# Routing of a mixture of experts: one number for each token, one-hots over the main blocks alone, and the first gathers inside the routing

## What is computed

```python
g_sel = jnp.argmax(g_logits, axis=-1)                  # one of 8 groups
top_p, top_i = lax.top_k(e_prob, 2)                    # two of its 8 experts
gate = g_gate * top_p / jnp.sum(top_p, axis=-1, keepdims=True)
expert = g_sel[:, None] * 8 + top_i
...
hb = jax.nn.silu(xb @ w1[e]) * (xb @ w3[e])            # xb: the rows of expert e
y = hb @ w2[e]
...
out = out.at[tok].add(y * gate)                        # each token gets two rows back
```

## Time and profile before

| | us |
|---|---|
| median of 3 runs | 3280.99 |
| lowest and highest | 3271.0, 3282.21 |
| the profiled execution | 3282.73 |
| its span, first to last instruction | 3280.9 |
| mean granted TensorE clock in it | 0.939 |

### The profile page before, as it was taken

One profiled execution on the slowest core, in us unless ns is written; L12 is line 12 of the kernel. 1 busy time (PEld: TensorE's weight loads), 2 busy tenths in 40 slices (PEclk: granted clock), 3 DMA queues, 4 the chain that ended last, 5 costly groups with the idle time before them and its releaser, 6 DMA issues. The chain is left out here.

```text
span 3280.9 us, 43057 instructions
## 1 busy us (share of the span) xinstructions
PE 2813.0 (86%) x16709; PEld 1832.8 (56%) x16709; DVE 1559.1 (48%) x2502; ACT 940.7 (29%) x1565; POOL 322.1 (10%) x388
## 2 busy tenths in 40 slices
PE   5999879897999999999999997698878766988785
PEld 3678778575888878865555576233222552333231
DVE  3148868558777766764555556011111571111114
ACT  6112322244322324444333432011001451111014
POOL 0000045300000000120101000111100001111100
PEclk8999989898999999999999997899999978999897
DMA  7511100212322338550000125899999759999996
GB/s 290 204 56 38 65 14 1 116 52 77 109 97 96 109 107 276 189 178 7 7 7 4 52 94 209 366 399 424 424 423 416 268 200 378 399 424 424 423 415 254
DMA packets 196700, 663.63 MB, mean 202 GB/s; under 512 B 42039, under 2 KB 83070, under 8 KB 142734
## 3 DMA queue, kind: packets, MB, share of 16 engines
q1 hardware_dynamic: 178062, 627.26, 49.0%
q0 software_dynamic: 18432, 33.60, 2.7%
HBM read 614.36 MB, written 79.95 MB: 212 GB/s over the span
## 5 line engine op out<-in xcount | busy, mean ns | idle before, releaser
L3131 PE MATMUL psum<-moe_ring,hreg 128*32 128x512 f32 x2976 | 482.8, 633 | 90.1 <-DMA moe_ring<-in_moe_w 48.2
L3131 PEld LDWEIGHTS psum<-moe_ring,hreg 128*32 128x32 f32 x2976 | 146.6, 116 | 386.4 <-issue 319.7
L3131 PE MATMUL psum<-x,hreg 128*32 128x512 f32 x896 | 319.8, 650 | 13.4 <-DMA moe_ring<-in_moe_w 13.4
L3237 DVE TENSOR_TENSOR ex_hb<-ex_sil,psum 128x256 f32<-128x256 f32 x64 | 27.0, 422 | 577.9 <-ACT ex_sil L3210 577.9
L3183 PE MATMUL psum<-moe_ring,hreg 128*32 128x512 f32 x1344 | 221.9, 599 | 16.6 <-issue 14.6
L1351 PE MATMUL psum<-gu_hi,x1r 128*128 128x512 f32 x712 | 226.6, 394 | 7.9 <-DVE x1r L1478 3.8
L1704 PE MATMUL psum<-dn_op 128*128 128x512 f32 x924 | 212.7, 393 | 4.3 <-DVE dn_op L1799 4.3
L1704 PEld LDWEIGHTS psum<-dn_op 128*128 128x128 f32 x924 | 175.3, 190 | 41.7 <-DVE dn_op L1799 5.1
L3210 ACT ACTIVATE ex_sil<-psum 128x256 f32<-128x256 f32 x64 | 24.6, 385 | 566.8 <-PE psum L3131 566.8
L1351 PE MATMUL psum<-gu_hi,gu_er 128*128 128x512 f32 x504 | 158.5, 389 | 0.0
L1351 PEld LDWEIGHTS psum<-gu_hi,x1r 128*128 128x128 f32 x712 | 135.4, 190 | 37.8 <-DVE gu_lo L1474 7.4
(11 more groups left out here) (643 smaller groups left out, 5893.3 us busy)
## 6 DMA issues: line engine op xcount, KB each, us to landing
moe_ring<-in_moe_w SPq DMA_DIRECT2D x256, 1024.0 KB, 19.2
x<-in_moe_w SPq DMA_DIRECT2D x96, 1024.0 KB, 21.6
moe_top<-in_moe_w SPq DMA_DIRECT2D x24, 1024.0 KB, 21.0
x<-in_w_down SPq DMA_DIRECT2D x77, 256.0 KB, 3.0
x<-midrow SPq DMA_DIRECT2D x77, 256.0 KB, 3.5
XF<-in_w_ada SPq DMA_DIRECT2D x16, 1024.0 KB, 6.2
moe_ring<-yrow SPq DMA_DIRECT2D x16, 1024.0 KB, 10.2
xrow<-x SPq DMA_DIRECT2D x24, 512.0 KB, 3.5
```

Of the source, the lines that this page charges most:

```text
L3131: last = pe.matmul(ps[i][r, :], xT[i][:, k, r], place[HOME[n, j]][:, kk * 512:(kk + 1) * 512], start=k == 0, stop=k == KD - 1)
L3237: dve.tensor_tensor(hb[i][:, :], sil[q % 2][:, :], ps[i][:, DE:2 * DE], ALU.mult).then_inc(hbd, 1)
```

## The change

Five things are changed in `routing`, and the parts that go with them.

- **One number for each token.** The constant table `C_TAB` goes. TensorE adds one more product to the sum in `ps[2]`: `code`, a constant of the rank, times `ranked_at`, a one-hot of each expert's rank. So `ps[2]` holds the token's rank in its low ten bits, and the place of its expert and the passes of its window above them. VectorE multiplies and sums once for each choice instead of twice, cuts the number into five fields with shifts and masks (`FI`, `F`), and block and row are sums of fields. A token without a place gets a block number out of range.
- **One-hots over 32 blocks.** The block one-hots of all 16 groups are made by one operation (`BO`, 512 columns), and two more weigh them with the two parts of the token's number (`BV`). They and the 16 row one-hots are bf16, each with a buffer of its own, so that nothing waits for a buffer. ScalarE makes none of them. TensorE has 16 bf16 products of 64 columns where 16 f32 ones of 96 were.
- **Overflow apart.** What served the further blocks alone (`Vrow`, `OC`, their one-hots and lists) moves to the new `overflow_routing`, under the same `nc.If`. `F` and `ovc` stay allocated until behind it, and so do the routing's buffers; the top places of the ring are named behind it.
- **First gathers.** The four first gathers are issued by GpSimd at the end of the routing block, when the list is there and the buffers are zeroed. `ranked_experts` starts with the fifth. The overflow branch issues them once more at its end, because it uses their buffers.
- **Idle products.** `keep_busy(pe, K, 0, 3)` ahead of the first turn goes. The gates' arithmetic (`GT`) moves from behind the one-hots to a place ahead of them.

```diff
+def gather(pool, K, q, place, sem):
+    pool.indirect_dma_start(place, None, K.xrow, bass.IndirectOffsetOnAxis(ap=K.GIDX[:, q:q + 1], axis=0),
+                            bounds_check=L - 1, oob_is_err=False).then_inc(sem, 16)
...
             @block.gpsimd
...
+                pool.wait_ge(zeroed, 4)
+                pool.wait_ge(gidx_ok, 1)
+                for q, xg in enumerate(gather_buffers(K)):
+                    gather(pool, K, q, xg, K.ga[q])
...
             @block.tensor
...
+                    if t == 2:
+                        pe.wait_ge(over_ok, 1)
+                        pe.matmul(ps[1][:, 0:NE], one[0:NE, :], over_it[:, :], start=True, stop=True).then_inc(over_mm, 1)
...
+                pe.wait_ge(at_ok, 1)
+                pe.matmul(ps[2][:, :].rearrange("p (t e) -> p t e", e=NE), code[:, :],
+                          ranked_at[:, :].unsqueeze(1).to_broadcast([P, NT, NE]), start=False, stop=True).then_inc(cmm, 1)
...
-                    pe.matmul(ps[6][:, 0:NB], RO[n % 4][:, :], BO[n % 4][:, :], start=n == 0, stop=n == 2 * NT - 1).then_inc(tmm, 1)
+                    last = pe.matmul(ps[6][:, 0:2 * MAIN], RO[:, n, :], BV[:, n, :, :].rearrange("p v b -> p (v b)"),
+                                     start=n == 0, stop=n == 2 * NT - 1)
...
             @block.vector
...
+                dve.tensor_scalar(ranked_at[:, :], ps[1][:, 0:NE], cst[:, C_COL + 2:C_COL + 3], None, ALU.is_equal).then_inc(at_ok, 1)
...
+                dve.tensor_tensor(BO[:, :, :], iota(MAIN).unsqueeze(1).to_broadcast([P, 2 * NT, MAIN]),
+                                  blf[:, :].unsqueeze(2).to_broadcast([P, 2 * NT, MAIN]), ALU.is_equal)
...
+                for n in range(2 * NT):
+                    dve.tensor_scalar(RO[:, n, :], numbers[:, :], rwf[:, n:n + 1], None, ALU.is_equal).then_inc(oh_ok, 1)
...
+                dve.tensor_single_scalar(K.GIDX[:, 0:MAIN], K.SIDX[:, 0:MAIN], 1, ALU.arith_shift_right).then_inc(gidx_ok, 1)
...
 def ranked_experts(nc, K, A, layer, tag, ctx, E):
...
-        for q in range(NG + passes[0]):
-            gather(q)
+        for q in range(NG, NG + passes[0]):
+            rows(q)
...
-        keep_busy(pe, K, 0, 3)
         turn_x(0)
...
 def moe(nc, K, A, layer, R, after):
...
         with nc.If(overflow > 0):
+            overflow_routing(nc, K, f"or{layer}_", R)
             experts(nc, K, A, layer, f"ov{layer}_", MAIN, OVER, [K.sem(f"ov{layer}_w{s}") for s in range(4)], 0)
```

More of the change, by code:

```diff
@@ L117, in constant_table @@
     t[:NE, C_COL + 1] = e
+    t[:, C_COL + 2] = i % NE
+    t[:NE, C_COL + 3] = 1024 * (e % GROUPS + GROUPS * np.array(FIRST_PASS)[e // GROUPS])
+    t[NE:, C_COL + 3] = 131072 * (passes - 1)
+    for k in range(2):
+        for m in range(NT):
+            t[:, C_VAL + 2 * (k * NT + m)] = 2 * i + k + 1
+            t[:, C_VAL + 2 * (k * NT + m) + 1] = 256 * m
     return t
@@ L2809, in routing @@
-        one, before = sb("one", [P, P], BF16), sb("before", [P, P], BF16)
-        sli, rwi, bli = (sb(n, [P, 2, NT], I32) for n in ("sli", "rwi", "bli"))
-        rwf, blf, nbl = sb("rwf", [P, 2, NT]), sb("blf", [P, 2, NT]), sb("nbl", [P, 2, NT])
-        ntk = sb("ntk", [P, 2 * NT])
-        RO = [sb(f"RO{i}", [P, P]) for i in range(4)]
-        BO = [sb(f"BO{i}", [P, NB]) for i in range(4)]
-        vt, v0 = sb("vt", [P, NB]), sb("v0", [P, NB])
-        BA = [sb(f"BA{n}", [P, NB]) for n in range(7)]
@@ L2817, in routing @@
-        exd, rmm, oh_ok, tmm, ones_ok = (K.sem(tag + n) for n in ("exd", "rmm", "oh_ok", "tmm", "ones"))
-        before_ok, cmm, block_ok, act_ok = (K.sem(tag + n) for n in ("before_ok", "cmm", "block_ok", "act_ok"))
-        by_act = range(3, 2 * NT, 2)
-        rank_ok, order_mm, order_ok, v_ok, v_mm, oe_ok, eo_mm = (K.sem(tag + n) for n in (
-            "rank_ok", "order_mm", "order_ok", "v_ok", "v_mm", "oe_ok", "eo_mm"))
+        one, before, code, numbers = (sb(n, [P, P], BF16) for n in ("one", "before", "code", "numbers"))
@@ L2852, in _ @@
                 for t in range(NT - 1):
-                    last = pe.matmul(ps[2][:, (t + 1) * NE:NT * NE].rearrange("p (t e) -> p t e", e=NE), one[:, :],
-                                     AS[:, t:t + 1, :].to_broadcast([P, NT - 1 - t, NE]), start=False, stop=t == NT - 2)
-                last.then_inc(cmm, 1)
+                    if t == 2:
+                        pe.wait_ge(over_ok, 1)
+                        pe.matmul(ps[1][:, 0:NE], one[0:NE, :], over_it[:, :], start=True, stop=True).then_inc(over_mm, 1)
@@ new lines, in _ @@
+                    pe.matmul(ps[2][:, (t + 1) * NE:NT * NE].rearrange("p (t e) -> p t e", e=NE), one[:, :],
+                              AS[:, t:t + 1, :].to_broadcast([P, NT - 1 - t, NE]), start=False, stop=False)
+                pe.wait_ge(code_ok, 1)
+                pe.wait_ge(at_ok, 1)
+                pe.matmul(ps[2][:, :].rearrange("p (t e) -> p t e", e=NE), code[:, :],
+                          ranked_at[:, :].unsqueeze(1).to_broadcast([P, NT, NE]), start=False, stop=True).then_inc(cmm, 1)
@@ L2871, in _ @@
+                last.then_inc(tmm, 1)
             @block.scalar
@@ L2966, in _ @@
+                dve.tensor_copy(blf[:, :], bli[:, :])
                 dve.drain()
[L2967 to L2974 removed]
@@ L3044, in ranked_experts @@
     hb = [sb(f"hb{i}", [P, DE]) for i in range(4)]
-    ga = [K.sem(tag + f"ga{i}") for i in range(NG)]
+    ga = K.ga
     sc = [K.sem(tag + f"sc{i}") for i in range(NY)]
@@ L3095, in gpsimd @@
                 for q in range(start[x + 1], end[x + 1]):
-                    gather(q + NG)
+                    rows(q + NG)
             for q in range(start[x], end[x]):
@@ L3343, in carry_wait, with gather_block @@
                     pool.tensor_tensor(scr[:, 0:1], scr[:, 1:2], scr[:, 1:2], ALU.add)
-                def gather(b, p, half):
+                def gather_block(b, p, half):
                     wait(pool, tx, b, -1, 2)
@@ L3376, in _ @@
                     pool.wait_ge(sc[i], 16 * count // 2)
+                for q, place in enumerate(gather_buffers(K)):
+                    gather(pool, K, q, place, rnew)
+                pool.wait_ge(rnew, 64)
             @block.tensor
@@ L3505, in moe @@
         K.last_in = [K.sem(f"moe{layer}_last{k}") for k in range(2)]
+        K.ga = [K.sem(f"moe{layer}_ga{i}") for i in range(len(gather_buffers(K)))]
+        chosen = ExitStack()
+        K.F = chosen.enter_context(nc.sbuf_tensor(f"moe{layer}_F", [P, 5, 2 * NT], F32))
+        K.ovc = chosen.enter_context(nc.sbuf_tensor(f"moe{layer}_ovc", [NE, 1], F32))
         routing(nc, K, A, layer, f"ro{layer}_", R)
-        R.ctx.close()
-        for i in range(AT_TOP):
-            with nc.sbuf_tensor(f"moe{layer}_top{i}", [P, PIECE], F32, side="right") as under:
-                K.place.append(under[:, :])
         overflow = nc.values_load(K.EO[0:1, OVER:OVER + 1], min_val=0, max_val=OVER)
@@ L3517, in moe @@
         with nc.If(overflow > 0):
+            overflow_routing(nc, K, f"or{layer}_", R)
             experts(nc, K, A, layer, f"ov{layer}_", MAIN, OVER, [K.sem(f"ov{layer}_w{s}") for s in range(4)], 0)
+        chosen.close()
+        R.ctx.close()
+        for i in range(AT_TOP):
+            with nc.sbuf_tensor(f"moe{layer}_top{i}", [P, PIECE], F32, side="right") as under:
+                K.place.append(under[:, :])
         E = Memory()
```

258 lines of the change are left out of this document (143 added, 115 removed).

## The result

| | median (us) | runs | lowest to highest | ratio to before, 95% interval |
|---|---|---|---|---|
| before | 3279.24 | 12 | 3271.0 to 3285.44 | |
| changed | 3286.72 | 12 | 3283.82 to 3289.87 | 1.0021 [1.0013, 1.0028] |

The changed kernel is **slower by about 7 us**, where 3268 was forecast; that is less than half a per cent, but the interval of the ratio leaves out 1. Its profiled execution took 3288.4 us, with a span of 3286.6 us. In that execution the routing starts a little earlier than in the one before, so I count from its first row (vrow: 2024.37 and 2685.1 us here, 2027.00 and 2686.4 before).

A forecast was written before the change was run, and what follows sets the result against it. Bound: the experts' weight stream, with one idle gap per layer, ceiling 16.8 us. Gains of 8.3 us in layer 0 and 4.6 in layer 1, rounded to 13, off the median 3281.0 gave 3268.0 us; range 3260 to 3279.

The forecast's parts named there:

- The bound: Experts' stage: its weight stream sets the end; routing gains only from one idle gap per layer, 16.8 us in all.
- The list: VectorE's routing chain: list done 15.6 us after its first row instead of 23.3, 7.7 us earlier.
- The front: VectorE's chain from first row to first wide product: 3.0 us instead of 3.7.
- the 16 row one-hots: VectorE in routing: 16 operations of 128 columns at 0.20 us each, 3.2 us; lower bound 1.6.
- The gathers ahead of the barrier: End of routing: four gathers take 5.4 us with hand-over, so 2.3 of 7.7 us reach the barrier.
- The rows come behind the ring: Rival, first turn: early gathers land only after the ring's loads, TensorE waits; 3281 to 3285 us, chance 0.06.
- TensorE's start: Barrier to TensorE's first weight load: kept at 6.7 us in layer 0 and 7.7 in layer 1.
- The second stop: TensorE behind its first load, layer 0: 5.3 us, taken as gone; its return in one layer a rival, 3272, chance 0.17.
- The idle products: First turn and first half product: without them the lower clock costs 2.2 us in each layer.
- The loads' old starts: Weight stream: loads restart at about 2063.8 instead of 2073.2 in layer 0, 2724 instead of 2729.5 in layer 1.
- over 6 us: Sign of a wrong forecast: a first half product in the experts' stage lasting over 6 us.

The follow-up runs named there:

- one_early: The changed kernel with only the first of the four gathers left in the routing block, the other three behind the branch; 3268.7 us.
- late_warm: The changed kernel with its four first gathers back behind the branch and the three idle products put back ahead of the first turn; 3264.1 us.
- quiet_early: The changed kernel with the loads of the first turn's weights moved behind the barrier, so its early gathers meet idle DMA engines; 3296.3 us.
- before_early: The kernel before with only its four first gathers moved into the routing block, idle products kept; 3296.0 us.
- early_warm: The changed kernel with only the three idle products put back ahead of the first turn; 3289.2 us.
- between_warm: The changed kernel with its four first gathers issued between barrier and branch, and the three idle products put back; 3260.1 us.

## Why the prediction was wrong

**The bound** was right: the stream of weights sets the end, and its gap is the currency.

**The list** was right in kind and a little small in size: 14.4 us behind vrow for a forecast of 15.6 (bounds 13.6 and 16.8). The front was 2.74 for 3.0, and the 16 row one-hots 2.69 for 3.2. The latter's pitch is 0.16 us against the 0.20 of f32, so bf16 helped by a fifth. The 1.6 us that the prediction worked out by the Trainium skill's table (VectorE: DVE Perf Modes, The perf-mode tier table), which is for 2048 columns, were not seen in these rows of 128, and the measurement decides.

**The gathers ahead of the barrier** is the step that failed: "They take 2056.52 + 0.99 - 2052.39 = 5.1 us, with the hand-over 5.4." and "So of the 7.7 us only **2.3 us** reach the barrier: 2048.0 instead of 2050.3." I saw that the barrier stands behind them and priced their issue. The price was their landing: 20.8 us from list to read of EO, not 5.4. GpSimd's Drain has no term in the sum. In the routing block of before it had no DMA of its own behind it and took 0.62 us. The trace of before has one other place with GpSimd's own DMAs ahead of a Drain, the end of the experts' block, L3524, which I did not use:

```profile
L3524 POOLq DRAIN  x2: 5429/5430/5432, 2566.1 to 3222.8; - x2
```

It is no landing that this one waits for: the program waits for the last scatter, issued at 2561.76 and landed 4.2 us later, before this Drain begins. Its length goes with the DMAs that GpSimd issued in the block: 5.43 us with 64 in all seven traces that have 64, 5.35 with 63 (`one_early`), 5.09 to 5.10 with 60 (the four traces with all real gathers in the routing block). That is 0.085 us each, an estimate from these rows, and 0.3 us for four, about what lies between the last landing and the Drain's end in the routing block (0.4 us at most). So it would not have given the price either, but it shows that 0.62 us was not the price of a GpSimd Drain with DMAs ahead of it.

The upper bound was in the same trace. The landing of 8.4 to 9.9 us behind the start of the last issue, 4.1 us after the first, puts the last landing at 2055.4 to 2056.9. And rows 8 show the first gather of four only; the fourth of that group, issued at 2113.64 with the DMA engines full, landed like this:

```profile
hreg<-xrow,GIDX POOLq DMA_INDIRECT x1, 15.2
```

With it the last landing stands at 2042.9 + 4.1 + 15.2 = 2062.2, and the barrier 12 us later than before instead of 2.3 us earlier; behind vrow it came 11.6 us later. A range with that in it would have had a rival on the slow side with a real chance.

**The rivals.** "The rows come behind the ring" was slower too, between 3281 and 3285, but by another road: its test was a first landing over 11.8 us, and the first landed after 8.7. The rows ran beside the ring's loads and the fourth landed after 15.3 us; what paid was not the turn of the first but the barrier. Its chance was 0.06, the range ended at 3279, and the time at 3286.7.

**TensorE's start.** I kept 6.7 and 7.7 us from barrier to first load; they were 5.1 and 4.3, with a DMA share of 0.16 and 0.05 meanwhile. With the engines full, in `late_warm`, it takes 7.4 and 6.3, and with them nearly idle, in `quiet_early`, 4.4 and 4.0, so the start goes with the load of the DMA engines. In the changed kernel the DMA engines carry, besides the start of the one top piece, five packets in each layer in this time, of the queues that the profile calls instruction (q8 and q14); that TensorE waits for those is not shown. The second stop went, and came back only in `before_early`, layer 0, which has the old routing code (5.25 us; `early_warm` and `late_warm` run the same idle products without it). That agrees with the prediction's guess that it hangs on the code ahead, but no run moved the code alone.

**The idle products.** 2.2 us of clock was about right: 2.5 in layer 0 of `early_warm`. With the gap closed no gain from the clock can be told (3260.1 for 3260.2 us).

**A slip in the sum.** The loads' old starts are given as 2073.2 and 2729.5; the trace has 2072.50 and 2728.73. The gains are worked out from differences and do not change.

**Still open**: a stop of 2.9 us in TensorE's weight loads within the first product of layer 1 in the changed kernel (up to 2729.87, "issue"), part of that layer's larger loss. It makes the first half of that product 8.3 us long, where the prediction named "over 6 us" as a sign of being wrong; in layer 0 it took 5.4. Open are also what GpSimd waits for behind the branch in layer 1, and what its Drain does for 0.085 us per DMA issued.

## What to carry to other kernels

Before a DMA issue is moved ahead of a barrier, ask what its engine must do to leave the block: on GpSimd the Drain at the end waited for the landing (0.7 us with no gather, 18 us with four), so an early gather turned a transfer that was hidden into a wait for all engines. Behind the barrier and ahead of the branch the same four gathers cost GpSimd 2 us that no engine was seen to wait for, and the kernel gained 21 us instead of losing 7. And an operation that the trace shows only in an easy state (a Drain with nothing under way) has only a lower bound there; the upper bound is the slowest thing that it could be waiting for, read from the last of a group and not from the first.

## What the hardware showed that was not expected

- GpSimd's Drain at the end of the routing block ends within 0.4 us of the landing of its last gather, wherever the trace has that landing: 9.0 us with one gather, 18.1 with four beside the ring's loads, 7.5 with four and idle DMA engines; with no gather it takes 0.6 to 0.7. (`before_early`, 9.9 us, has no landing for its last gather.) SyncE's Drain takes 0.12 us with its loads under way.
- At the end of the experts' block, with everything landed, GpSimd's Drain takes 5.43 us after 64 DMAs of its own, 5.35 after 63 and 5.09 to 5.10 after 60.
- A gather of which every row is out of bounds is not free: it lands after 2.1 to 2.3 us with idle DMA engines and 7.6 to 11.2 us beside the ring's loads, and an early one holds the Drain just the same.
- Gathers issued 1.3 us apart beside full DMA engines land ever later: 8.7, 10.8, 13.2 and 15.3 us after their issue; with idle ones 4.4 to 5.2. The trace of before had this too (8.4, 10.9, 13.0 and 15.2 for the group issued from 2109.34 on).
- TensorE's stop behind the branch is 4.0 to 5.1 us in the runs in which the DMA engines are nearly idle then (the changed kernel, `quiet_early`, `early_warm`, `before_early`) and 6.3 to 7.7 us with them full (before, `late_warm`, `between_warm`).
